# Hybrid encoder trunk on one core: gate batches moved to the 48 middle tiles, and the last groups' h kept in SBUF

## The chip, the cores and the metric

The kernel runs on one core of a Trainium2 chip. The metric is device time in microseconds (us) of one execution. TensorE is PE in the rows, its weight loads PEld, VectorE DVE, ScalarE ACT, GpSimd POOL, SyncE SP. DMA issues stand under the engine that issues them (SPq, ACTq, POOLq).

## The reference

An input of 512 tokens by 1024 goes through two layers. Each has a mixer (layer 0: differential attention beside a convolution module; layer 1: gated linear attention) and then a PEER block, which is where the change lies. Cut to the PEER block:

```python
def peer(h, w_query, sub_keys, expert_u, expert_v):
    def block(xb):
        q = (xb @ w_query).reshape(t, PEER_HEADS, 2, PEER_HALF)          # 8 heads
        scores = jnp.einsum('thpd,hpnd->thpn', q, sk)                    # 2 x 128 sub-keys
        s_val, s_idx = lax.top_k(scores, PEER_TOPK)                      # 16
        cand = s_val[:, :, 0, :, None] + s_val[:, :, 1, None, :]
        c_val, c_idx = lax.top_k(cand.reshape(...), PEER_TOPK)
        expert = i1 * N_KEYS + i2                                        # 128 * 128 experts
        gate = jax.nn.softmax(c_val, axis=-1)
        act = jax.nn.gelu(jnp.einsum('thkd,td->thk', expert_u[expert], xb))
        coef = gate * act
        return jnp.einsum('thk,thkd->td', coef, expert_v[expert])
```

## The kernel before, in words

Of the four blocks of 128 tokens the kernel treats the first one as the reference does: it gathers the chosen 128 rows of U (and later of V) per token by indirect DMA from POOL (`gather`, L437 to L444, a ring of NBUF = 5 rows of 512 KB), and DVE takes a dot product with each row of U (`dots`, L885) and adds each row of V times its coefficient to the residual (`sums`, L894). 128 dots come before 128 sums in a layer.

The other 384 tokens (TD) are computed densely, against all 16384 experts. PE runs 128 tiles of 128 experts: `tile` (L1269 to L1282) multiplies a tile of U with x, both split into a high and a low bf16 part, 24 matmuls. ACT applies Gelu to the result (`tile` on ACT, L609 to L618), which is h. U is loaded by SP four tiles (one group, 2048 KB) at a time (`stream_load`, L368 to L372); ACT makes the high part (`split_hi`, L591 to L596) and DVE the low part (`split_lo`, L849 to L854), both called by `ahead(n)`, four tiles ahead of PE's use. The ring of split tiles has eight places (RING), the raw groups have two. ACT stores h of each group to DRAM (`h_store`, L620 to L622, 768 KB in 128 rows).

A dense matrix of gates must be built for these tokens, as the experts times tokens, zero but for 128 experts per token. DVE makes one-hot rows for a batch of BT = 8 tokens (`hots`, L1002 to L1010), PE multiplies them (`batch` L1314 to L1325, 16 matmuls) and ACT copies the result out (`gates_out`, L645 to L656). There are NB = 48 batches. Four of them make a chunk of 32 tokens (NCK = 12 chunks); a finished chunk lies in one of two staging buffers `gst` (one of them over xnT), and ACT stores it to DRAM (L656, 2048 KB in rows of 512 bytes), all but the last chunk.

The stages of one PEER block follow one another, each engine running its own program with semaphores between them:

- Head stage: 64 tiles, eight per head; between them PE computes the queries (L1290) and scores (L1297) of a head and DVE its top-k (L897 to L977), with HEAD_DOTS = 7 dots per head from the second on, in two parts, before the wait for the scores and at the end of the head.
- The picks are transposed on PE (L1303 to L1312), the gate values normalized (Exp on ACT, L640; L984 to L988 on DVE), all of it between two tiles: PE runs nothing else here.
- Gate stage: 64 tiles; three of every four carry a batch, b = 3k + (n % 4), and DVE takes one dot per tile.
- Down stage: 32 groups of four tiles with V. For each, DVE multiplies h, read back from DRAM, by the gates (`group`, L1019 to L1032: 11 of 12 chunks from DRAM at L1026, the last from staging at L1029), ACT rounds the product to bf16 (L672), DVE subtracts to get the low part (L1032), then both split the next group's V, and PE adds 72 matmuls to the output in PSUM (L1338 to L1354). DVE adds V_DOTS = 5 dots or sums per group (dots before group HG_GROUP = 3, sums after). SP reads gates and h per group (`gh_load`, L384 to L388), each after the low part two groups before is done.

What orders the work around the change is written out by hand in each engine's program: a DMA issue or a wait on ACT or SP holds back everything behind it on that engine. PE may start tile n when Gelu of tile n - 2 is done and its split parts are there, and a batch when its one-hots are there (there are two buffers of them).

Of the kernel before, what the change touches and what calls it, by code (L numbers as in the profile page):

```python
# [8 lines left out]
F32 = mybir.dt.float32  # L9
# [6 lines left out]
P = 128  # L16
# [17 lines left out]
PH = 8  # L34
# [15 lines left out]
HEAD_DOTS = 7  # L50
V_DOTS = 5
HG_GROUP = 3
# [33 lines left out]
def build(nc, x_d, cols_d, const_d, hot_d, relb_d, wmix_d, wz_d, wg2_d, wq_d, u_d, ur0_d, ur1_d, v0_d, v1_d,  # L86
          gffn_d, lnf_d, out_d):
    gate_d = nc.dram_tensor("gate_scratch", [NG, P, NCK, TPG * CHK], F32).ap()
# [5 lines left out]
    with ExitStack() as ctx:  # L94
# [133 lines left out]
        gr = [view(at, NCK, TPG, CHK) for at in gr_at]  # L228
        grf = [view(at, NCK, TPG * CHK) for at in gr_at]
# [109 lines left out]
        def _(sp):  # L339
# [16 lines left out]
            def peer_loads(L):  # L356
# [34 lines left out]
                sp.wait_ge(g_out[0], 16 * (NCK // 2 * (L + 1) + 1))  # L391
                sp.wait_ge(g_out[1], 16 * ((NCK // 2 - 1) * (L + 1) + 1))
                sp.wait_ge(h_out[0], 16 * (16 * (L + 1) + 1))
                sp.wait_ge(h_out[1], 16 * (16 * (L + 1)))
                gh_load(0, 0)
                sp.wait_ge(h_out[1], 16 * (16 * (L + 1) + 1))
                gh_load(0, 1)
# [58 lines left out]
        def _(act):  # L456
# [141 lines left out]
            def peer(L):  # L598
# [10 lines left out]
                def tile(n, between=None):  # L609
                    c = n // TPG  # L610
                    ahead(n + TPG)
                    if n % TPG == 0:

                        act.wait_ge(h_out[c % 2], 16 * (16 * L + c // 2 + 1))
# [20 lines left out]
                for n in range(NK // 2):  # L635
                    tile(n, {1: queries_out, 2: scores_out}.get(n % RING))
                    if n % TPG == TPG - 1:
                        h_store(n // TPG)
                act.wait_ge(ge_sub, L + 1)
                act.activation(ex, ex, ACT.Exp).then_inc(ge_exp, 1)  # L640
                for k in range(2):
                    act.wait_ge(pick_tr, 3 * L + k + 1)
                    act.activation(pk[:, k], ps[:, 6, 0:TD], ACT.Copy).then_inc(pick_i, 1)

                def gates_out(b):  # L645
                    c, at = b // 4, 2 + 2 * (b % 2)
                    act.wait_ge(g_built, NB * L + b + 3)
                    if b % 4 == 0:

                        act.wait_ge(g_out[c % 2], 16 * ((NCK // 2 - c % 2) * L + c // 2 + 1))  # L650
# [3 lines left out]
                    if b % 4 == 3 and c < NCK - 1:  # L654
# [3 lines left out]
                for n in range(NK // 2, NK):  # L658
                    tile(n)
                    k, b = n // TPG - NK // 2 // TPG, n % TPG  # L660
                    if b < 3:
                        gates_out(3 * k + b)
                    if n % TPG == TPG - 1:
                        h_store(n // TPG)

                def group(g):

                    s = g % 2
                    act.wait_ge(cf_ready, NG * L + g + 1)

                    act.wait_ge(tile_used, T0 + NK + TPG * (g + 1))
                    act.activation(chi[s].rearrange("p a b -> p (a b)"), hst[s].rearrange("p a b -> p (a b)"),  # L672
                                   ACT.Copy).then_inc(chi_ready, 1)
                    if g + 1 < NG:
                        for q in range(TPG):
                            ahead(NK + TPG * (g + 1) + q)

                for g in range(NG):
                    group(g)
                    if g == HG_GROUP:  # L680
# [11 lines left out]
        def _(dve):  # L692
# [163 lines left out]
            def peer(L):  # L856
# [40 lines left out]
                for h in range(PH):  # L897
# [78 lines left out]
                    if h:  # L976
# [461 lines left out]
```

## Time and profile before

| | us |
|---|---|
| median of 3 runs | 3175.97 (3174.02 to 3177.83) |
| the profiled execution's own time | 3178.46 |
| its span in the trace | 3176.7 |

| engine | busy us | share |
|---|---|---|
| PE | 2949.6 | 93% |
| DVE | 2304.1 | 73% |
| ACT | 1009.0 | 32% |
| POOL | 665.8 | 21% |

The busy time of an engine is what its instructions took, without waits and without the issuing of DMAs. Matmuls are pipelined, so a mean duration per matmul is longer than the distance between two. The profiled execution lies 2.5 us above the median of the runs. In this trace the PEER block of layer 0 runs from some 330 to 1594 us (head stage to 710, gate stage from about 729 to 1053, down stage from 1065) and that of layer 1 from 1908 to 3164.

### The profile page before, as it was taken

How to read it: one execution, taken by the hardware profiler on the slowest of the kernel's cores; microseconds unless marked ns; L12 is line 12 of the kernel's file. 1: busy time of each engine (PE TensorE's matmuls, PEld its weight loads, DVE VectorE, ACT ScalarE, POOL GpSimd, SP SyncE). 2: the span in 40 equal slices, each digit the busy share in tenths (PEclk: the TensorE clock that was granted, in tenths of full speed). 3: DMA queues.
4: the chain of work that ended last, by engine and by line, in shares of the span. 5: the costliest groups of instructions: out<-in, count | busy, mean ns of one | idle time of the engine just before them, and what ended most of it. 6: DMA issues, size and time to landing. Idle time of an engine off the chain costs nothing.

```text
span 3176.7 us, 39546 instructions
## 1 busy us (share of the span) xinstructions
PE 2949.6 (93%) x14632; PEld 1552.2 (49%) x14632; DVE 2304.1 (73%) x4099; ACT 1009.0 (32%) x1300; POOL 665.8 (21%) x518
## 2 busy tenths in 40 slices
PE   8978999998989899999989989999899998999998
PEld 4434455555656444444444445555466663444443
DVE  3852688989878788888510236988988887888884
ACT  2051332234444333323331113332244442333233
POOL 0000022212222334443000001122122223334430
PEclk9968999998999999999989999999999998999999
DMA  3200466658989999999511114566588999999993
GB/s 141 80 27 0 190 236 217 234 213 278 314 309 317 362 380 378 374 380 377 195 54 65 68 53 188 223 231 217 214 286 322 335 325 366 377 379 377 374 381 114
DMA packets 218948, 790.38 MB, mean 249 GB/s; under 512 B 15509, under 2 KB 105753, under 8 KB 198474
## 3 DMA queue, kind: packets, MB, share of 16 engines
q1 hardware_dynamic: 45410, 423.92, 35.0%
q0 software_dynamic: 73728, 268.47, 22.8%
q10 hardware_dynamic: 99688, 96.48, 8.9%
q8 instruction: 63, 1.03, 0.1%
q14 instruction: 59, 0.48, 0.0%
HBM read 688.93 MB, written 99.88 MB: 248 GB/s over the span
## 4 chain that ended last, share of the span: by engine, by line
PE 54%; DVE 27%; ACT 5%; issue 4%; DVEq 4%; DMA 3%; ACTq 2%; PEld 1%; POOL 0%; PEldq 0%; SPq 0%
DVE x_res L894 10%; PE ps L1279 9%; PE ps L1280 9%; PE ps L1281 9%; DVE arena L854 7%; PE ps L1290 7%; PE ps L1112 5%; PE ps L1103 5%; PE ps L1129 3%; DVE arena L1026 3%; ACT arena L672 3%; DVEq L895 2%; DVE arena L1032 2%; ACTq L622 1%; PE ps L1323 1%
## 5 line engine op out<-in xcount | busy, mean ns | idle before, releaser
L1350 PE MATMUL ps<-arena 128*128 128x512 bf16 x4608 | 1010.8, 381 | 67.6 <-ACT arena L596 67.6
L854 DVE TENSOR_TENSOR arena<-arena 128x1024 bf16<-128x1024 f32 x512 | 607.7, 1219 | 209.0 <-ACT arena L596 117.5
L1350 PEld LDWEIGHTS ps<-arena 128*128 128x128 bf16 x4608 | 449.0, 98 | 629.3 <-ACT arena L596 91.7
L444 POOL DMA_INDIRECT arena<-in_ur,arena x256 | 328.0, 1281 | 1846.5 <-DVE arena L885 1036.4
L1279 PE MATMUL ps<-xnh,arena 128*128 128x384 bf16 x2048 | 674.7, 329 | 11.5 <-DVE arena L854 7.2
L1280 PE MATMUL ps<-xnl,arena 128*128 128x384 bf16 x2048 | 674.6, 329 | 0.0
L1281 PE MATMUL ps<-xnh,arena 128*128 128x384 bf16 x2048 | 673.9, 329 | 0.0
L596 ACT ACTIVATE arena<-arena 128x1024 bf16<-128x1024 f32 x512 | 518.6, 1046 | 107.5 <-PE ps L1281 45.6
L444 POOL DMA_INDIRECT arena<-in_v,arena x256 | 336.9, 1316 | 514.4 <-DVE x_res L894 434.5
L894 DVE SCALAR_TENSOR_TENSOR x_res<-arena,x_res 128x1024 f32<-128x1024 f32 x256 | 328.5, 1283 | 19.5 <-issue 0.4
L885 DVE CUSTOM_DVE_ANT_0 arena<-arena 128x1024 f32<-128x1024 f32 x256 | 306.3, 1219 | 22.9 <-DMA arena<-in_ur,arena 22.6
L672 ACT ACTIVATE arena<-arena 128x1536 bf16<-128x1536 f32 x64 | 94.9, 1483 | 675.7 <-DVEq L1030 675.7
L618 ACT ACTIVATE arena<-ps 128x384 f32<-128x384 f32 x256 | 125.7, 491 | 525.4 <-PE ps L1281 525.4
L1279 PEld LDWEIGHTS ps<-xnh,arena 128*128 128x128 bf16 x2048 | 202.3, 99 | 144.2 <-issue 17.4
L1281 PEld LDWEIGHTS ps<-xnh,arena 128*128 128x128 bf16 x2048 | 202.2, 99 | 136.3 <-issue 6.1
L1280 PEld LDWEIGHTS ps<-xnl,arena 128*128 128x128 bf16 x2048 | 202.1, 99 | 132.6 <-issue 10.4
L1290 PE MATMUL ps<-xnT,arena 128*128 128x512 f32 x512 | 222.3, 592 | 0.0
L1032 DVE TENSOR_TENSOR arena<-arena 128x1536 bf16<-128x1536 f32 x64 | 112.6, 1759 | 101.0 <-ACT arena L672 101.0
L1112 PE MATMUL ps<-arena,xnT 128*128 128x512 f32 x384 | 166.9, 597 | 0.0
L1290 PEld LDWEIGHTS ps<-xnT,arena 128*128 128x128 f32 x512 | 96.8, 190 | 115.8 <-issue 114.8
L1103 PE MATMUL ps<-xnT,arena 128*128 128x512 f32 (+1 forms) x336 | 147.2, 600 | 1.6 <-ACT xnT L480 1.6
L1323 PE MATMUL ps<-arena 128*128 128x128 bf16 x768 | 101.9, 223 | 34.1 <-DVE arena L1010 34.1
(179 smaller groups left out, 2271.9 us busy)
## 6 DMA issues: line engine op xcount, KB each, us to landing
arena<-in_u SPq DMA_DIRECT2D x64, 2048.0 KB
arena<-in_v SPq DMA_DIRECT2D x64, 2048.0 KB
h_scratch<-arena ACTq DMA_DIRECT2D x64, 768.0 KB
arena<-h_scratch SPq DMA_DIRECT2D x64, 768.0 KB, 7.7
arena<-gate_scratch SPq DMA_DIRECT2D x64, 704.0 KB, 5.7
arena<-in_wmix SPq DMA_DIRECT2D x15, 2048.0 KB, 7.5
gate_scratch<-xnT ACTq DMA_DIRECT2D x12, 2048.0 KB
gate_scratch<-arena ACTq DMA_DIRECT2D x10, 2048.0 KB
```

Source lines behind the costliest of these rows:

```text
L444: pool.indirect_dma_start(ring[n % NBUF], None, ur_d[L] if g < P else vr_d[L], at).then_inc(gat_in[n % NBUF], 16)
L596: act.activation(hi[:, s], raw[s // TPG][:, s % TPG], ACT.Copy).then_inc(hi_ready, 1)
L854: dve.tensor_tensor(lo[:, s], raw[s // TPG][:, s % TPG], hi[:, s], ALU.subtract).then_inc(lo_ready, 1)
L885: dve.tensor_tensor_reduce(row, row, xg, 1.0, 0.0, ALU.mult, ALU.add, hg[:, g:g + 1]).then_inc(gat_free, 1)
L894: dve.scalar_tensor_tensor(x[:, 0], row, cf[:, g:g + 1], x[:, 0], ALU.mult, ALU.add).then_inc(gat_free, 1)
L1103: last = pe.matmul(bank[0:cols_of], wblk[b % 2][:, kd, at], xnT[:, kd], start=kd == 0, stop=kd == KD - 1)
L1112: last = pe.matmul(bank, xnT[:, kd, at], wblk[b % 2][:, kd], start=kd == 0, stop=kd == KD - 1)
L1279: pe.matmul(ps[:, j % 2, 0:TD], uh, xnh[:, kd], start=kd == 0, stop=False)
L1280: pe.matmul(ps[:, j % 2, 0:TD], uh, xnl[:, kd], start=False, stop=False)
L1281: last = pe.matmul(ps[:, j % 2, 0:TD], ul, xnh[:, kd], start=False, stop=kd == KD - 1)
L1290: last = pe.matmul(ps[:, 2 + s], wq[:, kd, at], xnT[:, kd], start=kd == 0, stop=kd == KD - 1)
L1350: last = pe.matmul(ps[:, 2 + 2 * tt + dh], c, v[:, slot, dh * 512:(dh + 1) * 512], start=False, stop=end and q == TPG - 1 and c is cl)
```

## The change

The gate batches move from "three of every four tiles of the second 64" to the 48 tiles 72 to 119 (B0 = 72), one batch in each, with eight plain tiles on either side. The transposes of the picks and the normalization stand inside the first eight plain tiles instead of ahead of them. Two chunks of gates stay in staging (NST = 10 are stored), and h of the last two groups, 30 and 31, stays in SBUF; the down stage takes these two groups first, in the order 30, 31, 0, 1, ... On DVE one dot or sum moves between the product and the subtraction of a group. The dots are dealt out anew: nine per head (four in the last), one in two of three batch tiles, two in each of the last eight tiles, five per group of the down stage up to its fifth.

```diff
-HEAD_DOTS = 7
+NST = NCK - 2
+B0 = NK // 2 + 8
+HEAD_DOTS = 9
 V_DOTS = 5
-HG_GROUP = 3
+HG_GROUP = 5
...
-                    stream_load(v_d[L][:, s], NG + s, s)
-                def gh_load(i, s):
-                    g = i * 2 + s
-                    sp.wait_ge(clo_ready, NG * L + g + 1)
-                    sp.dma_start(grf[s][:, 0:NCK - 1], gate_d[g][:, 0:NCK - 1]).then_inc(gh_in[s], 16)
-                    sp.dma_start(hsf[s], h_d[g]).then_inc(gh_in[s], 16)
...
+                    stream_load(v_d[L][:, NG - 2 + s], NG + s, s)
+                def gates_load(g, s):
+                    sp.dma_start(grf[s], gate_d[g]).then_inc(gh_in[s], 16)
+                for s in range(2):
+                    sp.wait_ge(g_out[s], 16 * (NST // 2 * (L + 1) + 1))
+                gates_load(NG - 2, 0)
+                sp.wait_ge(g_read, NB * (L + 1) + 2)
+                gates_load(NG - 1, 1)
+                for s in range(2):
+                    sp.wait_ge(h_out[s], 16 * ((NG // 2 - 1) * (L + 1) + 1))
                 with sp.Fori(0, NG // 2 - 1) as i:
                     for s in range(2):
-                        stream_load(v_d[L][:, i * 2 + (2 + s)], i * 2 + (NG + 2 + s), s)
-                        gh_load(i + 1, s)
+                        stream_load(v_d[L][:, i * 2 + s], i * 2 + (NG + 2 + s), s)
+                        sp.wait_ge(clo_ready, i * 2 + (NG * L + s + 3))
+                        gates_load(i * 2 + s, s)
+                        sp.dma_start(hsf[s], h_d[i * 2 + s]).then_inc(gh_in[s], 16)
...
-                for n in range(NK // 2, NK):
-                    tile(n)
-                    k, b = n // TPG - NK // 2 // TPG, n % TPG
-                    if b < 3:
-                        gates_out(3 * k + b)
-                    if n % TPG == TPG - 1:
-                        h_store(n // TPG)
...
-                    if b % 4 == 3 and c < NCK - 1:
+                    if b % 4 == 3 and c < NST:
...
+                for n in range(NK):
+                    tile(n, {1: queries_out, 2: scores_out}.get(n % RING) if n < NK // 2 else None)
+                    if B0 <= n < B0 + NB:
+                        gates_out(n - B0)
+                    if n % TPG == TPG - 1 and n // TPG < NG - 2:
+                        h_store(n // TPG)
+                    if n == NK // 2 + 3:
+                        act.wait_ge(pick_tr, 3 * L + 1)
+                        act.activation(pk[:, 0], ps[:, 6, 0:TD], ACT.Copy)
+                        act.wait_ge(pick_tr, 3 * L + 2)
+                        act.activation(pk[:, 1], ps[:, 5, 0:TD], ACT.Copy).then_inc(pick_i, 1)
+                        act.wait_ge(ge_sub, L + 1)
+                        act.activation(ex, ex, ACT.Exp).then_inc(ge_exp, 1)
+                    if n == NK - 2:
+                        high(0)
...
-                    if h:
+                    if 0 < h < PH - 1:
                         dots(HEAD_DOTS - HEAD_DOTS // 2)
...
+                def scale(k):
+                    s, g = k % 2, (k + NG - 2) % NG
+                    if k < 2:
+                        dve.wait_ge(gelu_done, NK * L + TPG * (g + 1) + 2)
+                    dve.wait_ge(gh_in[s], (32 * (NG // 2) - 16) * L + 16 + 32 * (k // 2))
+                    h4 = hst[s].rearrange("p q (c t) -> p q c t", t=CHK)
+                    early = h4[:, :, 0:NST]
+                    dve.tensor_tensor(early, early, gr[s].rearrange("p c q t -> p q c t"), ALU.mult)
+                    dve.wait_ge(g_read, NB * (L + 1) + 2)
+                    for c in range(2):
+                        late = h4[:, :, NST + c]
+                        dve.tensor_tensor(late, late, gst[c][:, g].rearrange("p (q t) -> p q t", q=TPG), ALU.mult)
+                    dve.drain().then_inc(cf_ready, 1)
+                def low(k):
+                    dve.wait_ge(chi_ready, NG * L + k + 1)
+                    dve.tensor_tensor(clo[k % 2], hst[k % 2], chi[k % 2], ALU.subtract).then_inc(clo_ready, 1)
+                for n in range(NK // 2 + 3, NK):
+                    if B0 <= n < B0 + NB:
+                        hots(n - B0)
                     ahead(n + TPG)
-                    dots(1)
+                    if n == NK - 3:
+                        scale(0)
+                    if B0 <= n < B0 + NB:
+                        dots(1 if n % 3 else 0)
+                    elif n >= B0:
+                        dots(2)
+                low(0)
+                for k in range(NG):
+                    if k:
+                        scale(k)
+                        if k > HG_GROUP:
+                            sums(1)
+                        else:
+                            dots(1)
+                        low(k)
...
-                        dots(V_DOTS)
+                        dots(V_DOTS - 1)
...
-                        sums(V_DOTS)
+                        sums(V_DOTS - 1)
...
-                pe.wait_ge(topk_done, PH * (L + 1) + 1)
-                for k in range(3):
...
+                for j in range(RING):
+                    tile(0, NK // 2 + j)
+                    if j == RING // 2 - 1:
+                        pe.wait_ge(topk_done, PH * (L + 1) + 1)
+                        for k in range(2):
+                            for tt in range(GT, TT):
+                                last = pe.transpose(ps[:, 6 - k, (tt - GT) * P:(tt - GT + 1) * P], picks[:, k, tt], ident)
+                            last.then_inc(pick_tr, 1)
+                    if j == RING // 2:
+                        pe.wait_ge(ge_ready, L + 1)
...
-                with pe.Fori(0, 2) as i:
-                    for j in range(NK // 4):
-                        tile(i * (NK // 4), NK // 2 + j)
-                        if j % TPG < 3:
-                            batch(i * (NB // 2), j // TPG * 3 + j % TPG)
+                with pe.Fori(0, NB // RING) as i:
+                    for j in range(RING):
+                        tile(i * RING, B0 + j)
+                        batch(i * RING, j)
+                for j in range(RING):
+                    tile(0, NK - RING + j)
```

## Rows read from the trace of the kernel before

**Rows 1.** The page: busy us (share of the span) and instructions, PE.
```profile
PE 2949.6 (93%) x14632; PEld 1552.2 (49%) x14632; DVE 2304.1 (73%) x4099; ACT 1009.0 (32%) x1300; POOL 665.8 (21%) x518
```

**Rows 2.** Busy time by stretch; PE, PEld, DVE, ACT, POOL, then PEclk, DMA share, GB/s.
```profile
726.00:1036.00 310.00, 287.15 (x2175) 187.97 (x2176) 254.49 (x367) 136.42 (x170) 66.22 (x61) 0.95 0.88 308
1052.00:1102.00 50.00, 35.58 (x158) 15.50 (x155) 32.76 (x40) 14.12 (x14) 16.50 (x11) 0.90 0.98 385
```

**Rows 3.** Instructions in order of time, PE, head to gate: start, us, line, [idle before].
```profile
719.87 0.90 PE L1311 MATMUL ps<-const,arena 128*128 128x128 f32 x3 [9.62 <-DVE arena L969]
726.54 0.90 PE L1311 MATMUL ps<-const,arena 128*128 128x128 f32 x3 [5.77 <-ACT arena L643]
```

**Rows 4.** Order of time, ACT's queue: stores of h on either side of that boundary.
```profile
710.82 0.34 ACTq L622 DMA_DIRECT2D h_scratch<-arena  x1
749.10 0.34 ACTq L622 DMA_DIRECT2D h_scratch<-arena  x1
```

**Rows 5.** Order of time, ACT's queue, gate stage of layer 0: stores of gates (L656), h (L622).
```profile
777.62 0.39 ACTq L656 DMA_DIRECT2D gate_scratch<-arena  x1
785.80 0.34 ACTq L622 DMA_DIRECT2D h_scratch<-arena  x1
800.78 0.39 ACTq L656 DMA_DIRECT2D gate_scratch<-xnT  x1
804.15 8.68 ACTq L622 DMA_DIRECT2D h_scratch<-arena  x1
...
831.54 0.34 ACTq L622 DMA_DIRECT2D h_scratch<-arena  x1
```

**Rows 6.** The same view: the other long issues, both layers, and two rows beside one.
```profile
886.60 10.25 ACTq L622 DMA_DIRECT2D h_scratch<-arena  x1
...
971.26 8.60 ACTq L622 DMA_DIRECT2D h_scratch<-arena  x1
...
2381.00 8.75 ACTq L622 DMA_DIRECT2D h_scratch<-arena  x1
...
2460.16 0.39 ACTq L656 DMA_DIRECT2D gate_scratch<-arena  x1
2463.53 3.81 ACTq L622 DMA_DIRECT2D h_scratch<-arena  x1
2486.95 0.34 ACTq L622 DMA_DIRECT2D h_scratch<-arena  x1
...
2542.00 8.68 ACTq L622 DMA_DIRECT2D h_scratch<-arena  x1
```

**Rows 7.** DMA queues, 802 to 807 us (first row) and 809 to 812 (others): packets, MB.
```profile
q10 hardware_dynamic: 1830, 0.94, 75.9%
...
q1 hardware_dynamic: 64, 1.05, 81.5%
q10 hardware_dynamic: 66, 0.03, 3.7%
```

**Rows 8.** Order of time, PE, the first groups of the down stage.
```profile
1065.42 8.93 PE L1350 MATMUL ps<-arena 128*128 128x512 bf16 x32 [10.96 <-ACT arena L596]
...
1102.54 7.67 PE L1350 MATMUL ps<-arena 128*128 128x512 bf16 x27 [4.01 <-ACT arena L596]
```

**Rows 9.** Order of time, DVE, the products of one group of the down stage.
```profile
1294.97 1.63 DVE L1026 TENSOR_TENSOR arena<-arena 128x1408 f32<-128x1408 f32 x1
...
1298.38 1.76 DVE L1032 TENSOR_TENSOR arena<-arena 128x1536 bf16<-128x1536 f32 x1 [1.58 <-ACT arena L672]
```

**Rows 10.** Waits of PE, 1108 to 1540 us: total us, times, longest.
```profile
PE ps L1350 <- ACT arena L596: 19.3, 24, 1.2
```

**Rows 11.** Busy time by stretch, as rows 2: 24 groups of the down stage.
```profile
1130.00:1526.00 396.00, 377.49 (x1734) 167.71 (x1733) 346.66 (x288) 126.46 (x120) 156.35 (x120) 1.00 0.97 377
```

**Rows 12.** Waits over the whole span: DVE's for the copy of the scores.
```profile
DVE arena L854 <- ACT arena L632: 86.0, 15, 16.4
```

**Rows 13.** Order of time, SP's queue: the load of U beside the first long issue.
```profile
803.75 0.33 SPq L372 DMA_DIRECT2D arena<-in_u  x1
```

More of the change, by code:

```diff
@@ L227, in build @@
         gr_at = [A_GR, A_GR + TPG * TD]
-        gr = [view(at, NCK, TPG, CHK) for at in gr_at]
-        grf = [view(at, NCK, TPG * CHK) for at in gr_at]
+        gr = [view(at, NST, TPG, CHK) for at in gr_at]
+        grf = [view(at, NST, TPG * CHK) for at in gr_at]
         c_at = [A_X + 4096, A_X + 4096 + TPG * TD]
@@ L675, in group @@
+                for k in range(NG):
+                    if k:
+                        high(k)
+                    if k + 1 < NG:
                         for q in range(TPG):
[L676 to L680, printed above, removed]
+                            ahead(NK + TPG * (k + 1) + q)
+                    if k == HG_GROUP:
                         act.wait_ge(hg_ready, L + 1)
@@ L982, in peer @@
                 dve.tensor_tensor(ex, pv, top, ALU.subtract).then_inc(ge_sub, 1)
+                ahead(NK // 2 + 4)
                 dve.wait_ge(ge_exp, L + 1)
@@ L989, in peer @@
                                   erc.unsqueeze(2).to_broadcast([P, TT * PH, TOPK]), ALU.mult).then_inc(ge_ready, 1)
+                ahead(NK // 2 + 5)
+                ahead(NK // 2 + 6)
                 dve.wait_ge(pick_tr, 3 * L + 3)
@@ L1037, in peer @@
-                for g in range(NG):
-                    group(g)
-                    if g < HG_GROUP:
-                        dots(V_DOTS)
+                def scale(k):
[11 more added lines that the diff above has]
+                    dve.drain().then_inc(cf_ready, 1)
@@ new lines, in peer @@
+                low(0)
+                for k in range(NG):
+                    if k:
+                        scale(k)
[4 more added lines that the diff above has]
+                        low(k)
+                    if k + 1 < NG:
+                        for q in range(TPG):
+                            ahead(NK + TPG * (k + 1) + q)
+                    if k < HG_GROUP:
+                        dots(V_DOTS - 1)
@@ L1041, in peer @@
                     else:
-                        if g == HG_GROUP:
+                        if k == HG_GROUP:
                             dve.wait_ge(hg_act, L + 1)
@@ L1301, in peer @@
                         tile(h * RING, j)
-                pe.wait_ge(topk_done, PH * (L + 1) + 1)
-                for k in range(3):
-                    if k == 1:
-                        pe.wait_ge(pick_i, 2 * L + 1)
-                    if k == 2:
+                for j in range(RING):
[7 more added lines that the diff above has]
+                    if j == RING // 2:
                         pe.wait_ge(ge_ready, L + 1)
-                    for tt in range(GT, TT):
-                        src = picks[:, k, tt] if k < 2 else gt[:, tt]
-                        last = pe.transpose(ps[:, 6 + k // 2, (tt - GT) * P:(tt - GT + 1) * P], src, ident)
-                    last.then_inc(pick_tr, 1)
+                        for tt in range(GT, TT):
+                            last = pe.transpose(ps[:, 7, (tt - GT) * P:(tt - GT + 1) * P], gt[:, tt], ident)
+                        last.then_inc(pick_tr, 1)
                 def batch(first, b):
```

51 lines of the change are left out of this document (8 added, 43 removed).

## The prediction, made before the change was run

> **What bounds the kernel now.** I read the page's totals first [rows 1]: TensorE (PE) has work for 93% of the span, so a change can win only by closing holes on PE. The stretches show where they are [rows 2]: a granted clock of 0.95 over the gate stage, and 35.6 us of PE work in the 50 us after it. The instructions in order of time show two more, between the head and the gate stage and in every group of the down stage. Both layers look alike; I work out layer 0 and double, except for the stalls, which are counted one by one.
>
> *Head to gate.* After its 64th tile PE stands 9.62 us for the last head's top-k and 5.77 us between the transposes of the picks [rows 3]. The stores of h come once per four tiles, so their distance measures progress: 38.28 us over this boundary (710.82 to 749.10, [rows 4]) against 18.35 us (785.80 to 804.15, [rows 5]) for four tiles with three batches. The boundary costs 19.9 us, part of it a PE that restarts at a low clock.
>
> *Gate stage.* ScalarE (ACT) issues two kinds of store on one queue: gates (2048 KB) and h (768 KB). Issues take 0.34 to 0.39 us, but six stores of h took 8.68, 10.25, 8.60, 8.75, 3.81 and 8.68 us, 48.8 us in sum [rows 5, 6]. ACT does nothing else in that time. All six come 3.37 us after a gates store (804.15 against 800.78). The ones that come 8.2 us after (785.80 against 777.62) take 0.34. The reason is in the queues [rows 7]: in the five microseconds after a gates store its queue q10 moves 1830 packets, and once a load of experts (q1) runs beside it, 66 packets in three, one for one with q1's 64 far larger ones. A store is 4096 packets of 512 B, and I read the stall as h waiting behind those that have not yet gone out. The issue ends 12.05 us after that of the gates store (812.83 against 800.78), and in the six cases 12.05, 13.62, 11.97, 12.12, 7.18 and 12.05 us after, 11.5 on average (each h row's start and length, less its gates store, 3.37 us earlier). What a stall costs: 804.15 to 831.54 is 27.39 us, 9.0 over the 18.35, for one of 8.68; 2463.53 to 2486.95 is 5.1 over, for one of 3.81. So a stall costs its own length and some 0.6 us; the six cost 52.4 us.
>
> *Gate to down.* PE waits 10.96 us for the first group's h, which goes to DRAM and back, and 4.01 us more when gathers come late [rows 8]; a low clock over part of it I put at 4 us more.
>
> *Down stage.* The vector engine (DVE) repeats every 16.5 us (24 groups in the 396 us of [rows 11]), with 1.58 us of idleness for ACT's copy in each [rows 9]; PE waits 19.3 us in 24 groups, 0.80 each [rows 10], so PE's part is 15.7. But DMA is already busy 97% of that time at 377 GB/s [rows 11]; where it is saturated, before the stage, it moves 385 at 98% [rows 2].
>
> **The change, part by part** (against the profiled execution, 3178.5 us with a span of 3176.7; the median of the runs is 3176.0, 2.5 less).
>
> 1. *Eight plain tiles cover the pick.* PE has tiles 64 to 67 to run before it needs the picks, more than the 9.62 us that the last top-k still takes, so that wait goes; the five dots that stood behind the last head go elsewhere. Left on PE: nine transposes (2.7 us by 0.90 per three, [rows 3]) and a wait for the gate values, since two copies, a table load and Exp on ACT and then DVE's reduce, reciprocal and product follow one another with one tile (under 4.6 us, a quarter of 18.35) to hide them. In this order the trace does not show them; the bounds are nothing and the 5.77 us that PE stands there now, and as most of it is hidden I put 2 us. Of 19.9 us some 15 go. Bounds: 12 (nothing of the clock returns) and 18. Twice: **-30 us**.
>
> 2. *Two dots more per head* (9 for 7). Each 1.3 us; DVE waits for the scores 5.7 us per head (86.0 in 15, [rows 12]), which hides 2.6 us and a late gather. Nothing; without that cover up to 2.6 us for six heads.
>
> 3. *DVE in the gate stage* has two dots per three tiles instead of one per tile, the same four products for a batch: less work than PE's. Nothing.
>
> 4. *Last groups first in the down stage.* h of groups 30 and 31 never leaves SBUF, their gates are loaded during the last eight tiles; SP issues them ahead of V of group 0, whose load then waits on the completion of the gates and h stores, with eight tiles to spare. The copy of group 30 runs before the last tile. Of the 15 us and the low clock I keep 1 us. One more small product per group (0.28 us) is paid by a shorter main one (128x1280 for 128x1408). **-18 us** per layer, bounds 12 and 19.
>
> 5. *One dot or sum between product and subtraction* fills the 1.58 us. By DVE alone the period falls from 16.5 to about 15.2, by PE to 15.7. DMA decides: 377 GB/s over 16.5 us is 6.22 MB per group, of which only 64 KB (the eleventh chunk) go; 6.16 MB at 385 GB/s are 16.0 us. So 0.5 us for 25 groups: **-12 us** per layer. Bounds 4 (no better rate than 377, 0.17 us each) and 20 (PE's 15.7). The Trainium skill (DMA: Bandwidth & Descriptors, Bandwidth) names about 358 GB/s of HBM as the limit of a core; by it a group could not be had under 17.2 us and this term would be nothing. The trace's 377 is above it, so the measurement decides.
>
> Parts 4 and 5 together: -60 us over both layers.
>
> 6. *The stores.* A batch in each of 48 tiles closes a chunk at every fourth tile, n % 4 == 3, and that is the tile after which h is stored. All ten gates stores of a layer are now followed by a store of h at once, about 0.45 us after their issue, none 8 us after. The load of U for a later group is issued at the same place (DVE's last split of a group), so it runs beside the gates store, one packet for one. I take the release at the mean of the six, 11.5 us: a stall of 11.05 us, costing 11.65. What stands behind it: ACT's next split, then DVE's split, then the one-hots of the batch after next, then PE; PE has two tiles and two batches in hand, as now. Twenty times 11.65 is **+233 us**, and the present **-52.4** go. Bounds per stall: 6.7 us (the one release at 7.18) and 13.2 (the one at 13.62). The low end can also be nothing, see the rivals. The page Trace Analysis of the Trainium skill (DMA Instruction, HWDGE) says that the descriptor generator is locked until all of a transfer's descriptors are generated. By it the second store waits as I expect, but SP's load would wait too and the gates store itself would look long; here the gates store takes 0.39 us, so the trace agrees only in part.
>
> Sum: 3178.5 - 30 - 60 - 52.4 + 233 = 3269.1, less 2.5 for the median: **3267 us**.
>
> **Rivals.** *No stall (faster).* In the six cases SP had issued a load 0.4 us before the h that stalled (803.75 in [rows 13]). If it was the third transfer in line that had no room and not the second, h right behind gates is accepted at once. Then only the gains stay: 3178.5 - 142.4 - 2.5 = 3034 us. For it: the six all have that load. Against it: five of the six ended 12 us or more after the gates store, long after SP's load began to move, which a free place in a line does not explain. It decides if h is issued within 1 us. Chance 0.25.
>
> *Short stalls (level).* If nothing competes while ACT stands, each release comes at 7.18 as in the one short case: 20 x 7.33 = 147 us for 233, which gives 3180 us. For it: gathers stop when DVE stands. Against it: the load of U is issued before ACT stands. Chance 0.15, half of it on either side of the old time.
>
> *The down stage gains nothing* because DMA is full and what part 5 frees is lost to later gathers: its 24 us and the 16 us of waits for gathers and low clock come back, 3307 us. For it the 97%; against it the 385 that the row before the stage shows. Chance 0.1, within the forecast's side.
>
> **How the numbers follow.** The forecast itself, stalls of 9 to 13 us, 0.5; its own range 3215 to 3325. Within 0.2% (6.4 us, about what a measurement of this kernel tells from nothing) lies only a slice of the level rival, 0.03. Slower: 0.5 + 0.1 + 0.05, 0.65. Faster: 0.25 + 0.07, 0.32. As both signs hold weight, the range that leaves out 2 in 10 must take in the first rival: 3030 to 3325.
>
> **What would show it.** Right: twenty stores of h with issues of 8 to 13 us, each right behind a gates store; a distance of 29 to 33 us between h stores in the 48 middle tiles where PE needs some 19.3 (18.35 and a fourth batch, under 1 us); low granted clock in their wake; PE's wait before the first group of the down stage under 2 us, a group period of 16.0, and PE waiting under 3 us at the transposes. Wrong: h issues of 0.34 us in the gate stage; then the time is near 3034. If the period of a down group is 16.5 still, part 5 is; if PE waits for top-k, part 1 is.

## The result, and the profile after

The changed kernel takes **3266.23 us** (median of 4 runs, 3262.64 to 3268.12); the kernel before, beside it, 3176.47 (4 runs, 3174.02 to 3177.83). The ratio is 1.0282, 95% interval 1.0264 to 1.0300: slower by 90 us. The profiled execution took 3262.64 us with a span of 3260.8, and is the one read here.

The page of the changed kernel, its totals, the granted clock in 40 slices, and the chain of work that ended last:

```profile
PE 2972.5 (91%) x14632; PEld 1571.4 (48%) x14632; DVE 2316.6 (71%) x4163; ACT 1005.9 (31%) x1300; POOL 753.6 (23%) x518
...
PEclk9968999998888999999989999999988889999999
...
PE 63%; issue 10%; PEld 7%; ACTq 6%; DVE 5%; ACT 3%; DMA 2%; DVEq 2%; PEldq 1%; POOL 1%; SPq 0%; POOLq 0%
```

PE works 23 us more than before [rows 1] for the same number of instructions, so at a lower clock: 0.8 where the gate stages are. The new entry is "ACTq 6%": 6% of a chain of 3261 us is ScalarE's issuing. In order of time, ACT's queue at the end of the head stage and the start of the gate batches (L647 stores gates, L623 stores h):

```profile
710.54 0.34 ACTq L623 DMA_DIRECT2D h_scratch<-arena  x1
726.14 0.34 ACTq L623 DMA_DIRECT2D h_scratch<-arena  x1
746.58 0.34 ACTq L623 DMA_DIRECT2D h_scratch<-arena  x1
766.39 0.39 ACTq L647 DMA_DIRECT2D gate_scratch<-xnT  x1
766.82 9.26 ACTq L623 DMA_DIRECT2D h_scratch<-arena  x1
796.90 0.39 ACTq L647 DMA_DIRECT2D gate_scratch<-arena  x1
797.33 9.99 ACTq L623 DMA_DIRECT2D h_scratch<-arena  x1
```

Every one of the twenty h stores behind a gates store looks like that (ten per layer): 8.8 to 10.6 us in the issue, 195.4 us in sum, where [rows 5, 6] had six of them. The distance from h to h is 30.5 us here. The stretches (columns as in [rows 2]): the plain tiles around the picks, the batches, and 25 groups of the down stage:

```profile
705.00:726.00 21.00, 21.00 (x133) 12.90 (x132) 17.99 (x48) 7.67 (x11) 0.00 (x0) 1.00 0.46 179
766.00:1066.00 300.00, 215.58 (x1584) 141.08 (x1583) 175.68 (x250) 95.00 (x120) 29.78 (x26) 0.84 0.64 211
1130.00:1526.00 396.00, 392.48 (x1805) 177.10 (x1803) 360.81 (x348) 134.71 (x126) 189.75 (x123) 0.99 0.99 391
```

The middle row is the loss: PE has work for 72% of 300 us at a granted clock of 0.84, and DMA is far from full. The outer two rows are gains against before: no hole at the end of the head, and PE busy 99% of the down stage against 95% in [rows 11]. What PE waited for between 770 and 1066 us (total, times, longest):

```profile
PE ps L1344 <- DVE arena L1013: 84.4, 10, 9.4
```

These are ten waits, one per stall, for the one-hots. PE ran dry two steps behind ACT: ACT's split comes first, then DVE's split, then the one-hots, then PE's batch.

### The profile page after: what moved, and what is told of

It is laid out like the page before. It is cut to its first block, busy times and chain, and to the rows that moved or that the text cites. A ratio compares the mean times of both kernels' runs of the same rounds, so it can differ in the third digit from the quotient of the medians.

```text
span 3260.8 us, 39630 instructions
## 1 busy us (share of the span) xinstructions
PE 2972.5 (91%) x14632; PEld 1571.4 (48%) x14632; DVE 2316.6 (71%) x4163; ACT 1005.9 (31%) x1300; POOL 753.6 (23%) x518
## 4 chain that ended last, share of the span: by engine, by line
PE 63%; issue 10%; PEld 7%; ACTq 6%; DVE 5%; ACT 3%; DMA 2%; DVEq 2%; PEldq 1%; POOL 1%; SPq 0%; POOLq 0%
PE ps L1372 12%; PE ps L1297 8%; PE ps L1298 8%; PE ps L1299 8%; PEld ps L1372 7%; PE ps L1308 7%; ACTq L623 6%; PE ps L1130 5%; PE ps L1121 5%; PE ps L1147 3%; PE ps L1344 1%; PE ps L1345 1%; DMA arena<-in_ur,arena 1%; DVE arena L854 1%; DVEq L1011 1%
## 5 line engine op out<-in xcount | busy, mean ns | idle before, releaser
L445 POOL DMA_INDIRECT arena<-in_ur,arena x256 | 355.9, 1390 | 2004.9 <-DVE arena L885 1179.0
L1372 PEld LDWEIGHTS ps<-arena 128*128 128x128 bf16 x4608 | 452.5, 98 | 577.1 <-issue 30.0
L1297 PE MATMUL ps<-xnh,arena 128*128 128x384 bf16 x2048 | 683.4, 334 | 8.3 <-DVE arena L854 7.0
L1298 PE MATMUL ps<-xnl,arena 128*128 128x384 bf16 x2048 | 682.0, 333 | 0.0
L1299 PE MATMUL ps<-xnh,arena 128*128 128x384 bf16 x2048 | 680.9, 332 | 0.0
L445 POOL DMA_INDIRECT arena<-in_v,arena x256 | 396.8, 1550 | 412.8 <-DVE x_res L894 349.9
L1344 PE MATMUL ps<-arena 128*128 128x128 bf16 x768 | 113.3, 236 | 169.7 <-DVE arena L1013 169.7
L1344 PEld LDWEIGHTS ps<-arena 128*128 128x128 bf16 x768 | 81.0, 106 | 182.3 <-DVE arena L1013 177.4
## 6 DMA issues: line engine op xcount, KB each, us to landing
arena<-in_v SPq DMA_DIRECT2D x64, 2048.0 KB, 10.2
```

What stands on the lines that cost most here:

```text
L445: pool.indirect_dma_start(ring[n % NBUF], None, ur_d[L] if g < P else vr_d[L], at).then_inc(gat_in[n % NBUF], 16)
L1297: pe.matmul(ps[:, j % 2, 0:TD], uh, xnh[:, kd], start=kd == 0, stop=False)
L1298: pe.matmul(ps[:, j % 2, 0:TD], uh, xnl[:, kd], start=False, stop=False)
L1299: last = pe.matmul(ps[:, j % 2, 0:TD], ul, xnh[:, kd], start=False, stop=kd == KD - 1)
L1372: last = pe.matmul(ps[:, 2 + 2 * tt + dh], c, v[:, slot, dh * 512:(dh + 1) * 512], start=False, stop=end and q == TPG - 1 and c is cl)
```

## The experiments

**1. h ahead of gates.** The two statements of the tile loop change places:

```diff
-                    if B0 <= n < B0 + NB:
-                        gates_out(n - B0)
                     if n % TPG == TPG - 1 and n // TPG < NG - 2:
                         h_store(n // TPG)
+                    if B0 <= n < B0 + NB:
+                        gates_out(n - B0)
```

> The only edit to the changed kernel: at every fourth tile ACT stores h before it copies out and stores the gates, so h is ahead of the gates store and the next issue on ACT's queue comes a group later. Theory 1 (an issue on ACT's queue waits until the small rows of a gates store ahead of it in the same queue have gone out to some 1400 of 4096): no issue over 1 us, the twenty losses of some 10.9 us (a group takes 30.2 us where PE needs 19.3) go, and the kernel takes 3266 - 218 = 3048 us, faster than before. Theory 2 (a third transfer in line finds no room; SP's load of U and the gates store are the first two): now the gates store is the third, behind the load of U and h, and its issue is the long one, 4 to 10 us; time 3100 to 3260. Theory 3 (the gates stores load the DMA engines, whatever the order): within 1% of 3266.

Measured: 3042.89 us (3042.59 to 3043.18), against the kernel before in the same job 0.9565 (0.9538 to 0.9592). ACT's queue of this kernel in order of time:

```profile
761.95 0.34 ACTq L623 DMA_DIRECT2D h_scratch<-arena  x1
763.40 0.39 ACTq L647 DMA_DIRECT2D gate_scratch<-xnT  x1
781.22 0.35 ACTq L623 DMA_DIRECT2D h_scratch<-arena  x1
782.67 0.39 ACTq L647 DMA_DIRECT2D gate_scratch<-arena  x1
```

Not one issue of ACT in the gate stage is over 0.4 us, with the same transfers, and h follows h every 19.27 us. Here SP's load of U is issued first (761.06), then h, then gates, and the gates store as the third of three transfers issued in 2.3 us is taken at once. Two stretches of the same kernel, batches and down stage:

```profile
766.00:950.00 184.00, 184.00 (x1539) 124.91 (x1536) 170.38 (x245) 95.03 (x115) 29.84 (x26) 1.00 0.98 333
1130.00:1450.00 320.00, 320.00 (x1485) 145.07 (x1483) 301.32 (x268) 112.35 (x105) 158.33 (x102) 1.00 1.00 396
```

PE is never without work in either stretch, at full granted clock. So the whole loss hangs on which of the two stores is issued first: 3266.23 - 3042.89 = 223.3 us, or 11.17 per stall.

**2. h one tile later.** h of a group is issued at the end of the next tile, 2.93 us behind gates instead of 0.43:

```diff
+                    if n % TPG == 0 and 0 < n // TPG <= NG - 2:
+                        h_store(n // TPG - 1)
                     if B0 <= n < B0 + NB:
                         gates_out(n - B0)
-                    if n % TPG == TPG - 1 and n // TPG < NG - 2:
-                        h_store(n // TPG)
```

> The changed kernel with each store of h one tile later: after the Gelu of the next tile, some 4.2 us after the gates store instead of 0.4. Theory 1: the release stays where it is, 9.7 to 10.5 us after the gates store, so the issue takes some 6 us instead of 10; each group gains the 4 us, 20 x 4 = 80 us, about 3186 us. Theory 2: by then the load of U has left the line, no long issue, about 3048 us. Theory 3: no change, 3266.

Measured: 3164.38 us (3160.68 to 3167.58), ratio 0.9945 (0.9928 to 0.9961). Two pairs of its queue:

```profile
762.94 0.39 ACTq L647 DMA_DIRECT2D gate_scratch<-xnT  x1
765.87 6.20 ACTq L623 DMA_DIRECT2D h_scratch<-arena  x1
...
810.21 0.39 ACTq L647 DMA_DIRECT2D gate_scratch<-xnT  x1
813.14 9.15 ACTq L623 DMA_DIRECT2D h_scratch<-arena  x1
```

The end of the issue stays 8.4 to 12.3 us behind the gates store (772.07 - 762.94 = 9.1; 822.29 - 810.21 = 12.1), where it was 9.3 to 11.0 us in the changed kernel, although h is issued 2.5 us later; the twenty issues sum to 142.0 us. The release belongs to the gates store. The time is 22 us below the 3186 expected. The price of a stall is not a constant, though: (3164.38 - 3042.89) / 20 = 6.1 us for a mean issue of 7.1, less than its length, where in the changed kernel 11.2 is paid for 9.8.

**3. Half the rows.** The gates stores leave out the upper half of the groups (2048 rows for 4096, and so half the bytes), and the loads are pointed at what is there. Half of the groups get gates that are not theirs; the kernel serves to time the stores alone. Cut:

```diff
-gate_d = nc.dram_tensor("gate_scratch", [NG, P, NST, TPG * CHK], F32).ap()
+gate_d = nc.dram_tensor("gate_scratch", [NG // 2, P, NST, TPG * CHK], F32).ap()
...
-                        gates_load(i * 2 + s, s)
+                        gates_load(i + s, s)
...
-                        act.dma_start(gate_d[:, :, c].rearrange("g p q -> p g q"), gst[c % 2]).then_inc(g_out[c % 2], 16)
+                        act.dma_start(gate_d[:, :, c].rearrange("g p q -> p g q"), gst[c % 2][:, 0:NG // 2]).then_inc(g_out[c % 2], 16)
```

> The changed kernel with half of each gates store left out: only 16 of the 32 groups of a chunk are stored, 2048 rows of 512 bytes for 4096, and the down stage reads all its groups from these 16, so the gates of half the groups are not their own; the bytes read are as many as before. Theory 1: the release comes when some 1400 rows are left, so 2048 fewer must go out, at 680 per us some 3 us less: issues of some 7 us instead of 9 to 10.5, and 20 x 3 = 60 us less, 3206 us. Theory 2: the line is as long, the issue stays 9 to 10.5 us. Theory 3: half the store's load goes, issues unchanged, less than 30 us gained.

Measured: 3184.13 us (3179.24 to 3187.29), ratio 1.0011 (0.9993 to 1.0029). The issues fall to 5.24 to 6.89 us, 119.6 in sum: 3.8 us less each, not half, and not nothing. Next to it stands what the queues had moved between a gates store and the end of the h issue. First the changed kernel from 766.40 to 776.08 (packets, MB, share of 16 engines), then this one from 766.03 to 772.19:

```profile
q10 hardware_dynamic: 3197, 1.64, 55.7%
q1 hardware_dynamic: 123, 1.75, 46.7%
```

```profile
q1 hardware_dynamic: 123, 1.75, 76.4%
q10 hardware_dynamic: 744, 0.38, 20.4%
```

ACT was released when 4096 - 3197 = 899 rows of 512 B were left in the one, 2048 - 744 = 1304 in the other. The same count over the short stall of the kernel before, 2460.16 to 2467.34 (issue of 3.81 us in [rows 6]), and over its stall at 804.15:

```profile
q10 hardware_dynamic: 2431, 1.24, 66.1%
...
q10 hardware_dynamic: 2656, 1.36, 43.2%
```

There 1665 and 1440 were left. These four are single stalls. Over all twenty of the changed kernel the rows left run from 803 to 1271, and over all twenty with half the rows from 1076 to about 1900. One stall of each, from 917.45 to 928.42 and from 820.40 to 826.82 (4096 - 3293 = 803 left, the fewest, and 2048 - 161 = 1887, near the most):

```profile
q10 hardware_dynamic: 3293, 1.69, 50.7%
...
q10 hardware_dynamic: 161, 0.08, 4.2%
```

So ACT goes on while part of the store is still to go, but there is no one number of rows left at which it does. What sets the moment stays open; how long it takes depends on what runs beside it. In the first 4.6 us behind the gates store of the changed kernel (766.40 to 771.00) the load of U moved nearly alone:

```profile
q1 hardware_dynamic: 105, 1.72, 96.2%
q10 hardware_dynamic: 13, 0.01, 0.5%
```

Rows or bytes? Halving the rows halved both. The changed kernel has a comparison on SP's queue, shown further down: the load of V at 1100.77 moves 2048 KB too, but in 128 rows of 16 KB, and the two issues 0.43 us behind it take 0.86 us together. As many bytes in few rows hold nobody, there in a load and on the other engine's queue.

**4. h from SP's queue.** In the second half of the tiles SP issues the stores of h, behind its load of U; ACT issues gates as before:

```diff
+                        sp.wait_ge(gelu_done, h * 8 + (NK * L + 4 * s + 2))
+                        sp.dma_start(h_d[h * 2 + (s - 1)], hsf[1 - s]).then_inc(h_out[1 - s], 16)
...
-                    if n % TPG == TPG - 1 and n // TPG < NG - 2:
+                    if n % TPG == TPG - 1 and n // TPG < NG // 2 - 1:
```

> The changed kernel with the stores of h of groups 15 to 29 issued by SP, behind its load of U, instead of by ACT; the gates stores stay on ACT's queue. Theory 1, own queue: SP's queue holds no small rows, so SP's issues stay at 0.33 us and ACT never stands; about 3048 us. If instead the generator of descriptors is held by the gates store for whoever comes next, SP's issue of h is the long one (8 to 10 us), but PE loses little, since SP's next load is due only 15 us later: 3048 to 3080 us. Theory 3: 3266.

Measured: 3043.48 us (3043.19 to 3043.78), ratio 0.9567 (0.9532 to 0.9602). SP's queue in order of time:

```profile
780.67 0.33 SPq L374 DMA_DIRECT2D arena<-in_u  x1
781.79 0.35 SPq L384 DMA_DIRECT2D h_scratch<-arena  x1
```

SP is never held, with the gates store issued by ACT at 783.10 (0.38 us) and the one before at 763.83. This kernel equals experiment 1 in time (two executions). In it h is issued 1.3 us ahead of gates, so by itself it does not show an issue of SP right behind a gates store. The kernel before has one such issue at each of its six stalls: SP's load of U takes 0.33 us at 803.75 [rows 13], 3.0 us behind the gates store of 800.78. At the same distance, 2.93 us, all twenty issues of ACT in experiment 2 were held for 5.4 to 9.4 us. No run has an issue of SP while ACT is being held.

**5. and 6. The six stalls of the kernel before.** First h one tile later there too, ahead of that tile's gates:

```diff
+                    if b == 0 and k:
+                        h_store(n // TPG - 1)
                     if b < 3:
                         gates_out(3 * k + b)
-                    if n % TPG == TPG - 1:
-                        h_store(n // TPG)
```

> The kernel before with each store of h in the gate stage one tile later, ahead of that tile's gates: none then comes 3.4 us behind a gates store, the nearest is 8.2 us behind. Theory 1 (room in ACT's queue): the six long issues and their 52 us go, 3176 - 52 = 3124 us, the gate stage otherwise as it was. If the six were not what the low clock and the idle PE of the gate stage came from: under 10 us gained.

Measured: 3162.3 us (3158.74 to 3167.84), ratio 0.9943 (0.9921 to 0.9966), some 17 us of the expected 52. The edit missed its aim, none nearer than 8.2 us: four stores of h now come 6.83 us behind a gates store and are held for 6.1 to 7.2 us, with the release some 13.5 us behind:

```profile
801.79 0.39 ACTq L656 DMA_DIRECT2D gate_scratch<-xnT  x1
808.62 6.63 ACTq L622 DMA_DIRECT2D h_scratch<-arena  x1
```

Three more are held for 5.53, 2.80 and 1.93 us. The one of 2.80 us (at 2435.47) stands 11.65 us behind its gates store, when only some 170 rows of it are left and rows of h itself have begun to move, beside a load of U. Many rows left is therefore not the only thing that can hold an issue; what held this one was not traced.

Then the gates stores themselves, only those three per layer that stood 3.37 us ahead of h, issued behind it:

```diff
-                    if b % 4 == 3 and c < NCK - 1:
+                    if b % 4 == 3 and b % 3 < 2:
+                        g_store(b)
...
                     if n % TPG == TPG - 1:
                         h_store(n // TPG)
+                        if k % 4 == 3:
+                            g_store(3 * k + 2)
```

> The kernel before, with one change in the order of ACT's program: the three gates stores of a layer that a store of h used to follow 3.37 us later are now issued right behind that store of h instead of ahead of it; the other eight stay where they are, 8.2 us or more ahead of the next store of h. If a large-row gates store only blocks the next issue on its own sequencer, no issue of ACT in the gate stage is over 0.4 us, the distance between stores of h is 18.3 us throughout, and the time falls by the 52.4 us that the prediction put on the six stalls, to 3126. If instead the stalls of the kernel before came from the load of U that stands beside them, the h stores keep some long issues and the gain is under 20 us. If h right ahead of the gates makes the gates' own issue wait, an issue at L656 or its successor shows it.

Measured: 3136.37 us (3129.06 to 3147.35), ratio 0.9876 (0.9846 to 0.9905); by the medians 3179.43 - 3136.37 = 43 us (the interval allows 30 to 49), by the profiled spans 3176.7 - 3130.9 = 45.8. Where h stood 8.68 us, its queue now has

```profile
804.10 0.34 ACTq L622 DMA_DIRECT2D h_scratch<-arena  x1
804.48 0.59 ACTq L661 DMA_DIRECT2D gate_scratch<-xnT  x1
```

and h follows h every 18.35 us. The load of U is beside it as it was, so it is not what holds ACT. One issue is still 2.57 us and one 1.46, in layer 1. The six stalls cost some 43 to 46 us; in layer 0 the last store of h comes 27.7 us earlier (1026.02 for 1053.73), and PE then waits 6.82 us for a split of V at 1075.84, where [rows 8] had 4.01.

**7. The down stage's fill, alone.** In the kernel before, one dot or sum moves between the product and the subtraction of every group but the first:

```diff
+                    if g > HG_GROUP:
+                        sums(1)
+                    elif g:
+                        dots(1)
...
-                        dots(V_DOTS)
+                        dots(V_DOTS - (g > 0))
...
-                        sums(V_DOTS)
+                        sums(V_DOTS - 1)
```

> The kernel before with one dot or sum of each group of the down stage moved between the product and the subtraction, the rest as it was (part 5 alone). Theory A (DMA sets the down stage, at the 385 GB/s I took): the group period falls from 16.5 to 16.1 us, some 24 groups in two layers: 17 to 20 us gained, 3157. Theory B (DVE set it and DMA can give the 391 to 396 GB/s that the changed kernel's stretches show): the period falls to PE's 15.6, some 43 us gained, 3133.

Measured: 3127.98 us (3118.96 to 3138.39), ratio 0.9832 (0.9793 to 0.9870), so 52 us less, with 41 to 66 in the interval. DVE's products of two groups in order of time, and the stretch 1130 to 1520:

```profile
1295.31 1.62 DVE L1026 TENSOR_TENSOR arena<-arena 128x1408 f32<-128x1408 f32 x1
...
1310.85 1.62 DVE L1026 TENSOR_TENSOR arena<-arena 128x1408 f32<-128x1408 f32 x1
```

```profile
1130.00:1520.00 390.00, 388.69 (x1783) 176.81 (x1807) 364.30 (x301) 135.63 (x127) 184.97 (x119) 1.00 0.99 394
```

The period is 15.54 us, not 16.0: PE is busy for 388.7 of 390 us, and DMA moves 394 GB/s at 0.99 of its time. A DMA share of 0.97 at 377 GB/s [rows 11] was not its ceiling.

**8. The picks ahead of the plain tiles.** Experiment 1, with the transposes of the picks (not those of the gate values) where they had been, before the first of the eight plain tiles (both blocks of the pick moved up, in front of the loop):

```diff
+                pe.wait_ge(topk_done, PH * (L + 1) + 1)
+                for k in range(2):
+                    for tt in range(GT, TT):
+                        last = pe.transpose(ps[:, 6 - k, (tt - GT) * P:(tt - GT + 1) * P], picks[:, k, tt], ident)
+                    last.then_inc(pick_tr, 1)
                 for j in range(RING):
                     tile(0, NK // 2 + j)
-                    if j == RING // 2 - 1:
...
```

> The swapped kernel (h ahead of gates) with the transposes of the picks and their wait for the last top-k put back ahead of the first plain tile; the transposes of the gate values stay inside the plain tiles. If the plain tiles hide the top-k as part 1 says: PE stands some 9 us again in each layer and restarts at a low clock, 9 to 14 us per layer, 3043 + 18 to 28 = 3061 to 3071 us. If the tiles only moved the wait: under 5 us.

Measured: 3076.32 us (3072.45 to 3077.33), ratio 0.9673 (0.9647 to 0.9699): 33 us above experiment 1. PE stands 12.47 us at 722.57, and over the whole span

```profile
PE ps L1324 <- DVE arena L969: 23.0, 2, 12.5
```

so 23 us are the wait itself (two waits, one per layer); the other 10 were not traced to single rows.

**9. The gates of the first groups, ahead of V.** Experiment 1, with SP's loads of the gates of groups 30 and 31 issued before V's first two groups instead of behind them:

```diff
+                for s in range(2):
+                    stream_load(v_d[L][:, NG - 2 + s], NG + s, s)
```

(put behind the gates loads, and taken away ahead of them).

> The swapped kernel with SP loading the gates of groups 30 and 31 ahead of V of these groups. In the swapped kernel DVE waits 7.2 us for these gates (issued 0.4 us behind the second V load, at 989.4, though the gates were stored by 955) and PE 10.2 us after its last tile. If SP's order is what holds them: these 10 us per layer go, 3043 - 20 = 3023 us. If the gathers of the dots fill DMA in that stretch anyway: PE's wait moves to the next group and less than 8 us are gained.

Measured: 3036.01 us (3032.51 to 3037.13), ratio 0.9544 (0.9518 to 0.9570), the fastest version here. The gates are loaded 34 and 13 us earlier, yet PE still waits at the start. Its waits for DVE's low part over the whole span, in experiment 1, and then in this one (total, times, longest):

```profile
PE ps L1372 <- DVE arena L1033: 28.1, 4, 10.2
```

```profile
PE ps L1371 <- DVE arena L1032: 17.3, 4, 5.1
```

10.8 of 28.1 us of wait went, and the whole came out 6.9 us faster, for 20 expected. What holds the rest can be read from the trace, though no run changes it. ACT has rounded group 30 at 1004.86, PE has its last tile behind it at 1008, and DVE takes the low part only at 1011.17, without having been idle just before it:

```profile
1003.38 1.48 ACT L654 ACTIVATE arena<-arena 128x1536 bf16<-128x1536 f32 x1
1011.17 1.82 DVE L1032 TENSOR_TENSOR arena<-arena 128x1536 bf16<-128x1536 f32 x1
```

Between its product for group 30 and this low part DVE's program has the six dots of the last three tiles.

## Why the prediction was right

The direction and the mechanism were forecast: the twenty stalls, their length, 27 to 31 us between stores of h, and a low granted clock in their wake. That the time agrees within 1 us (3267 for 3266.23) is luck. Against the measured terms the stores were put 10 us too high, the present stalls 9 us too high, parts 4 and 5 together 11 us too high and part 1 3 us too low, and the measured terms themselves do not quite add up.

- **Part 6, the stores: the mechanism holds, the size was 4% over.** Predicted 20 × 11.65 = +233. Experiment 1 gives 223.3. The release came 9.77 + 0.43 = 10.2 us behind gates on average, not 11.5; the surcharge on the issue's own length was 1.4 us per stall, not 0.6. The granted clock of 0.84 over the stage is a likely reason; no run separates it. The rival *no stall* fell: right behind gates h stood each time. Its reading, that the third transfer in line has no room, is not answered by that, since SP's load of U was issued 2.4 us ahead of the gates store in the changed kernel too (764.04 and 766.39); experiment 1 answers it, where the gates store is the third and is taken in 0.39 us. The rival *short stalls* fell: in the first 4.6 us the load of U takes the engines and the gates rows hardly move. It was right that this load counts, by how it delays the rows. It does not move "one packet for one" with them, as part 6 has it, but ahead of them (105 packets for 13).
- **The present stalls, -52.4: too large.** Experiment 6 gives 43 to 46. Their length was right; in its trace time won before the down stage is partly lost at its start, and two issues of 4.0 us in sum remain.
- **Part 1, eight plain tiles: right.** From 710.54 to 746.58 are 36.04 us for eight tiles, against 31.2 for eight plain ones (twice 15.60), so 4.8 us stay on PE and of 19.9 us 15.1 go; 4.7 had been left. PE, in order of time, has no wait at the transposes of the picks and 1.17 us at those of the gate values, as "most of it is hidden" said:

```profile
725.42 0.82 PE L1327 MATMUL ps<-const,arena 128*128 128x128 f32 x6
...
731.31 0.55 PE L1332 MATMUL ps<-const,arena 128*128 128x128 f32 x3 [1.17 <-DVE arena L989]
```

  Experiment 8 puts hiding the picks at 33 us for both layers, where 30 were predicted for the whole part.
- **Part 2 and 3, more dots per head: nothing,** as said. PE has no gap from 705 to 726.
- **Part 4, the last groups first: failed.** It was to keep 1 us of the 15, and PE was to wait under 2 us before the first group; it waits 9.54. The first rows of the down stage, PE in order of time, and DVE's product ahead of them, in the changed kernel:

```profile
1128.17 8.05 PE L1372 MATMUL ps<-arena 128*128 128x512 bf16 x26 [9.54 <-DVE arena L1033]
...
1149.67 10.70 PE L1372 MATMUL ps<-arena 128*128 128x512 bf16 x41 [3.52 <-ACT arena L597]
```

```profile
1114.97 1.49 DVE L1024 TENSOR_TENSOR arena<-arena 128x1280 f32<-128x1280 f32 x1 [6.54 <-DMA arena<-gate_scratch]
```

  13.1 us of waits against 15.0 in [rows 8]. The step "their gates are loaded during the last eight tiles, with eight tiles to spare" was wrong: SP's program has V of group 31 ahead of both gates loads, and that load needs a raw buffer that comes free only as the last tiles are split. SP's queue in order of time:

```profile
1084.69 0.34 SPq L374 DMA_DIRECT2D arena<-in_v  x1
1100.77 0.34 SPq L374 DMA_DIRECT2D arena<-in_v  x1
1101.20 0.86 SPq L387 DMA_DIRECT2D arena<-gate_scratch  x2
```

  The h stays in SBUF, and it is the gates that come late. A queue that the moved step stands behind was not costed. Nor were the six dots that DVE's program puts between product and low part of group 30 (the product at 1114.97, the low part at 1126.17): by experiment 9 the first wait is still 5.1 us when the gates come early.
- **Part 5, the fill: right in kind, half its size.** Predicted 0.5 us per group, -24 for both layers; experiment 7 gives 3180 - 3128 = 52. The step "DMA decides: 385 GB/s, 16.0 us" took the best rate seen for the highest there is. Here it is 391 at 0.99, and the period 1314.69 - 1299.14 = 15.55:

```profile
1299.14 1.49 DVE L1024 TENSOR_TENSOR arena<-arena 128x1280 f32<-128x1280 f32 x1
...
1314.69 1.49 DVE L1024 TENSOR_TENSOR arena<-arena 128x1280 f32<-128x1280 f32 x1
```

  The bound by PE (15.7) was the one that held. The prediction took about 358 GB/s from the Trainium skill (DMA: Bandwidth & Descriptors, Bandwidth) as a core's limit. The same section gives that figure for two cores of a pair streaming at once, and 425 GB/s for a large transfer with one core alone. This kernel runs on one core, and its 391 over 396 us, and 396 over 320 us in experiment 1, lie between the two. Together parts 4 and 5 gave 24.7 us per layer for 30: the down stage with its first wait takes 1633.2 - 1118.6 = 514.6 us (from the end of the clearing of PSUM behind the last tile to the end of the last group), against 1593.75 - 1054.46 = 539.3. With the 52 us of experiment 7 for part 5, where 24 were predicted, next to nothing is left for part 4, where 36 were: the one error covered most of the other, and 11 of the 60 us are missing.

The sum of the measured terms, -33 - 49 - 43 + 223 = +98, is 8 us over the 90 found: the terms were taken one at a time, in different kernels, and are not quite additive. By the same experiments the gains alone are worth 3042.89 - 3179.9 = -137 us (-142.4 predicted, and 3034 us for a kernel without stalls).

What a stall costs beyond its own length is settled only roughly: 11.2 us for 9.8 right behind gates, 7.1 for 6.0 with half the rows, but 6.1 for 7.1 one tile later. Where in a group of four tiles ACT is held may matter; no run varied that alone.

## What to carry to other kernels

A DMA issue can be as cheap as 0.4 us and still close its queue to the next one for 10 us. Count the rows of a store and not only its bytes, and issue what others wait for ahead of the many-row transfer, or on another engine's queue. The order of two neighbouring statements was worth 223 us here, more than the 137 that the whole change gains without it. When a load is moved earlier, look at everything that stands ahead of it in its engine's program, and at which buffer that one needs; and a share of 97% on an engine is not yet its limit.

## What the runs showed of the hardware

The issue of the store of 4096 rows takes 0.39 us; what is long is the next issue on the same engine's queue, 8.8 to 10.6 us when it comes 0.43 us later. It ends before the store is complete, and neither after a fixed time (5.7 to 14.1 us behind the gates store) nor at a fixed number of rows left (803 to 1665 of 4096 in the changed kernel and the kernel before, 1076 to about 1900 of 2048 in experiment 3). SP's issue 3.0 us behind such a store takes 0.33 us. A store of 128 rows (h, 768 KB) did not hold the gates store issued 1.45 us behind it (0.39 us), and hardly one issued 0.38 us behind it (0.59 us in experiment 6). The Trainium skill (Perfetto Trace Analysis, DMA Instruction, HWDGE) holds the generator to be locked until a transfer's descriptors are made; the trace agrees in that a second transfer waits, and not in who waits or in which instruction shows the time. Not tried: how the release moves with the size of the rows, since only their number was halved.

In the changed kernel a queue with large packets nearly starved another queue's small rows: 105 packets of q1 (1.72 MB) for 13 of q10 in 4.6 us. The one packet for one of [rows 7] (64 and 66) is therefore not a fixed share.
